# Attention output formed transposed in a pipe of three steps, and the SSD half of the output projection moved ahead of the attention half

## The reference, cut to what matters

```python
def block_attention(q, k, v):            # 8 heads of 64, 2 key/value heads
    s = jnp.einsum('bqkgd,bskd->bkgqs', qi, k).astype(jnp.float32) * scale
    p = jax.nn.softmax(s, axis=-1).astype(v.dtype)
    return jnp.einsum('bkgqs,bskd->bqkgd', p, v)
...
attn = rms_norm(block_attention(q, k, v), attn_norm[i])
ssm = ssm_branch(z, xbc, dt_raw, ...)    # last: y * silu(z), then a grouped rms_norm with gain
x = x + jnp.concatenate([attn, ssm], axis=-1) @ w_out[i]
x = x + moe_ffn(rms_norm(x, norm_ffn[i]), w_router[i], ...)
```

## Time and profile before

| what | value |
|---|---|
| median of 3 runs | 1429.33 us |
| profiled execution, its own time | 1428.61 us |
| span of its records | 1426.8 us |
| TensorE busy | 1316.1 us (92%) |
| VectorE, ScalarE, GpSimd busy | 449.8, 218.2, 191.2 us |
| mean granted TensorE clock | 0.973 of 2.4 GHz |
| read from and written to HBM | 433.30 MB, 14.94 MB |

### The profile page before, as it was taken

How to read it: one execution, slowest core, us unless ns; L and a number is a source line. 1 busy time by engine, 2 the same in 40 slices (tenths; PEclk the granted TensorE clock), 3 DMA queues, 4 the chain that set the end, 5 groups by cost and what they waited for, 6 DMA issues and landing times.

```text
span 1426.8 us, 40195 instructions
## 1 busy us (share of the span) xinstructions
PE 1316.1 (92%) x18053; PEld 811.1 (57%) x18053; DVE 449.8 (32%) x1049; ACT 218.2 (15%) x487; POOL 191.2 (13%) x142
## 2 busy tenths in 40 slices
PE   5999989998799999999998988998999998999973
PEld 3466676665456666666565554655655654666651
DVE  3653577545322222222221221322221321322310
ACT  2132244331101101100110010110010011001100
POOL 0000210000101221111121111121121122012111
PEclk9999999998799999999999999999999999999996
DMA  8000320006999999999999999999999999999992
GB/s 348 4 1 0 148 107 1 31 30 246 384 373 373 394 391 380 403 383 400 395 397 402 396 412 399 407 403 393 411 396 404 406 399 410 389 415 381 407 404 84
DMA packets 79359, 446.18 MB, mean 313 GB/s; under 512 B 13226, under 2 KB 21490, under 8 KB 30034
## 3 DMA queue, kind: packets, MB, share of 16 engines
q1 hardware_dynamic: 63922, 425.85, 74.1%
q0 software_dynamic: 15120, 17.20, 5.7%
q10 hardware_dynamic: 144, 0.52, 0.1%
HBM read 433.30 MB, written 14.94 MB: 314 GB/s over the span
## 4 chain that ended last, share of the span: by engine, by line
SPq 43%; PE 43%; DMA 7%; issue 2%; DVE 2%; POOL 1%; ACT 0%; DVEq 0%; POOLq 0%; ACTq 0%
SPq L609 43%; PE pair L1832 19%; PE pair L1580 7%; DMA ring<-in_w_down 4%; PE pair L1564 4%; PE pair L1541 2%; DMA rest<-in_w_gate 2%; PE pair L1732 2%; PE pair L1672 2%; PE pair L1694 1%; PE pair L1791 1%; POOL ring L711 1%; DMA rest<-normed_rows,rest 1%; DVE rest L1038 1%; PE pair L1767 1%
## 5 line engine op out<-in xcount | busy, mean ns | idle before, releaser
L1832 PE MATMUL pair<-ring,rest 128*32 128x256 f32 x14832 | 847.1, 383 | 44.6 <-DMA ring<-in_w_down 23.6
L1832 PEld LDWEIGHTS pair<-ring,rest 128*32 128x32 f32 x14832 | 479.3, 110 | 358.4 <-issue 29.1
L751 POOL DMA_INDIRECT out<-rest x82 | 128.3, 1565 | 776.8 <-ACT rest L995 722.2
L1038 DVE TENSOR_TENSOR rest<-pair,rest 128x512 f32<-128x512 f32 (+4 forms) x113 | 88.9, 787 | 440.0 <-PE pair L1832 424.5
L995 ACT ACTIVATE rest<-rest 128x256 f32<-128x256 f32 x82 | 36.5, 500 | 541.4 <-DVE rest L1038 541.4
L1580 PE MATMUL pair<-ring 128*128 128x512 f32 (+1 forms) x256 | 99.8, 548 | 1.4 <-DVE ring L1038 0.8
L1580 PEld LDWEIGHTS pair<-ring 128*128 128x128 f32 x256 | 48.9, 193 | 48.3 <-issue 44.7
L1038 DVE TENSOR_TENSOR rest<-rest 128x512 f32<-128x512 f32 (+7 forms) x98 | 62.8, 651 | 32.6 <-ACT rest L977 26.7
L977 ACT ACTIVATE rest<-rest 128x512 f32<-128x512 f32 (+3 forms) x34 | 24.4, 718 | 299.5 <-DVE rest L1367 299.5
L1832 PE MATMUL pair<-rest 128*32 128x256 f32 x912 | 56.2, 384 | 6.5 <-DMA rest<-in_w_down 4.3
L1334 DVE TENSOR_SCALAR rest<-pair 64x1 int32<-64x1 f32 (+3 forms) x34 | 5.2, 152 | 176.0 <-issue 172.4
(11 more groups left out here) (177 smaller groups left out, 873.6 us busy)
## 6 DMA issues: line engine op xcount, KB each, us to landing
ring<-in_w_up SPq DMA_DIRECT2D x121, 1024.0 KB, 28.4
ring<-in_w_gate SPq DMA_DIRECT2D x120, 1024.0 KB, 28.8
ring<-in_w_down SPq DMA_DIRECT2D x120, 1024.0 KB, 29.3
rest<-in_w_gate SPq DMA_DIRECT2D x8, 1024.0 KB, 29.2
rest<-in_w_down SPq DMA_DIRECT2D x8, 1024.0 KB, 29.0
rest<-in_w_up SPq DMA_DIRECT2D x7, 1024.0 KB, 27.8
ring<-in_w_in SPq DMA_DIRECT2D x1, 4160.0 KB, 15.3
ring<-in_x SPq DMA_DIRECT2D x8, 512.0 KB, 6.0
```

Source lines behind the costliest of these rows:

```text
L751: p.indirect_dma_start(out=out_rows, out_offset=bass.IndirectOffsetOnAxis(ap=sidx[vi.ring][:, g:g + 1].bitcast(I32), axis=0), in_=yrow_b[v ...
L1038: return v.tensor_tensor(out=out, in0=a, in1=b, op=op)
L1832: last = T.matmul(ps[q * TOK:(q + 1) * TOK, g * QW:(g + 1) * QW], x, pieces[slot][:, kk, q * QW:(q + 1) * QW], start=(k == 0 and g % 2 == ...
```

## The change

- `attend` swaps the operands: 64 columns of values are stationary and 128 columns of transposed probabilities move; the two heads of a pair go to partitions 0-63 and 64-127 of bank 7, in turns. The attention output so arrives transposed. The pipe has one step more (PT, PV): probabilities are transposed two steps after their scores and used three steps after.
- The sums of the softmax are inverted, spread over 512 columns (`rsq`), transposed by TensorE (`rs`, 4 transposes) and copied out by ScalarE; VectorE multiplies bank 7 by them. The attention norm comes from squares (ScalarE) that TensorE adds with 4 one-column products (`an`); it is applied when VectorE adds the product to x1. The attention gain is multiplied into `w_out`'s first half by GpSimd.
- The output projection is split: the SSD half (`os`, 2 x 4 products) at steps 6, 9, 12, 15, the attention half (`op`, 2 x 4 products) at steps 8, 12, 16, 20. `combine` is at steps 2, 5, 8, 11. x1 is written by two additions per half.
- The sigmoids of z move ahead of the last copy of the SSD stretch, their product with z goes to GpSimd, and `carry_back` goes behind the first maxima. `choose` runs earlier; `th`a is no longer inside `op`b.
- Buffers lie elsewhere, and pieces are issued in another order: 0 to 3 before the loop, 4 to 7 after `yf3` and `op0`, 8 after `th1b`, 9 and 10 after `os3`, 11 and 12 after the last transposes and products of the attention, 13 and 14 after the last x1 tile, 15 and 16 after the last logits. `w_out` comes in two halves, the first behind `w_in`. The stores of the normalized rows are issued by ScalarE.
- Behind the last expert the handling of overflow rows waits in another place; no waiting row is added or taken away for the inputs here.

The diff, cut to its core (indented less):

```diff
-RING_AT = (0, 1, 16, 4, 5, 14, 15, 6, 7, 8, 9, 12, 13, 2, 3, 10, 11)
+RING_AT = (0, 1, 12, 13, 16, 4, 5, 6, 2, 7, 8, 14, 15, 10, 11, 3, 9)
...
-TM, OP, TH, LG = 7, 8, 9, 10
-STEPS = LG + 4 * (NT - 1) + 1
-
-
-def turn_at(s, first):
-
-    t, r = divmod(s - first, 4)
+PT, PV = 2, 3
+YO, TS, OS = 1, 4, 6
+RS, OP, TH, LG = 5, 8, 9, 10
+STEPS = LG + 4 * (NT - 1) + 2
...
+    if n == 2:
+        sp.dma_start(w_out_a, w_out_d[:, 0:KT // 2, :]).then_inc(s_woa, 16)
...
+sp.dma_start(w_out_s, w_out_d[:, KT // 2:KT, :]).then_inc(s_wos, 16)
 for t in range(NT):
     sp.dma_start(x1[:, t, :], x_d[t]).then_inc(s_xr[t], 16)
-sp.dma_start(w_out, w_out_d).then_inc(s_wout, 16)
+wait_full(sp, f"tk{NT - 1}")
...
+load(2, 0)
+load(3, 0)
+
+def store(t):
+
     wait_taken(sp, f"op{t}a")
     wait_taken(sp, f"op{t}b")
     sp.dma_start(out_d[t * P:(t + 1) * P, :], x1[:, t, :]).then_inc(s_ost, 16)
-    if t == NT - 1:
-        for n in range(7, 13):
-            load(n, STREAM[n][1])
-    if t < NT - 1:
-        sp.wait_ge(s_h, t + 1)
-        sp.dma_start(hn_d[t * P:(t + 1) * P, :], hrw).then_inc(s_hst, 16)
+
+store(0)
+sp.wait_ge(s_ys, NT)
+wait_full(sp, f"yf{NT - 1}")
+for n in (4, 5, 6, 7):
+    load(n, STREAM[n][1])
+store(1)
+sp.wait_ge(s_h, 2)
+wait_full(sp, "th1b")
+sp.wait_ge(s_ost, 16 * 2)
+load(8, STREAM[8][1])
+wait_full(sp, f"os{NT - 1}b")
+for n in (9, 10):
+    load(n, STREAM[n][1])
+store(2)
+wait_full(sp, f"p{NPAIR - 1}b")
+load(11, STREAM[11][1])
+sp.wait_ge(s_of, NPAIR)
+load(12, STREAM[12][1])
+store(NT - 1)
+for n in (13, 14):
+    load(n, STREAM[n][1])
 
 sp.wait_ge(s_ost, 16 * NT)
 sp.wait_ge(s_hst, 16 * NT)
 wait_full(sp, f"lg{NT - 1}")
-for n in (13, 14, 15, 16):
+for n in (15, 16):
...
+for n in range(KT // 2):
+    nc.gpsimd.tensor_tensor(out=w_out_a[:, n, :], in0=w_out_a[:, n, :],
+                            in1=pc_att[:, n:n + 1].to_broadcast([P, DM]), op=ALU.mult).then_inc(s_wog, 1)
...
+for c in range(NT):
+    pool.wait_ge(s_zsig, c + 1)
+    nc.gpsimd.tensor_tensor(out=zs[:, c, :], in0=zs[:, c, :], in1=xc[:, c, :], op=ALU.mult).then_inc(s_zg, 1)
...
+    if c == NT - 1:
+        for n in range(NT):
+            nc.scalar.activation(xc[:, n, :], zs[:, n, :], ACT.Sigmoid).then_inc(s_zsig, 1)
...
+    if (i := turn_at(s, RS, 4)) is not None:
+        if i:
+            act.wait_ge(s_ofree, i)
+        copy_out(f"rs{i}", rsT)
+    if (i := turn_at(s, RS + 2, 4)) is not None:
         act.wait_ge(s_ofree, i + 1)
-        link(nc.scalar.activation(junk, mixa, ACT.Square, accum_out=nss[:, 0, i:i + 1]))
-        rms(nrs[:, 0, i:i + 1], nss[:, 0, i:i + 1], AW).then_inc(s_an, 1)
-    if turn_at(s, 3) is not None:
-        i = turn_at(s, 3)
+        nc.scalar.activation(sqT, mixaT[i % 2].rearrange("p a b -> p (a b)"), ACT.Square).then_inc(s_sq, 1)
...
+def carry_back():
+
+    link(tt(by_head(ytmp[0]), by_head(prevb[2]), over(ex[:, 2, 40:48], HD)))
+    link(tt(prevb[1], prevb[1], ytmp[0], ALU.add))
+    link(tt(by_head(ytmp[0]), by_head(prevb[1]), over(ex[:, 1, 40:48], HD)))
+    tt(prevb[0], prevb[0], ytmp[0], ALU.add).then_inc(s_prev, 1)
+    dve.wait_ge(s_prev, 1)
...
+    if (i := turn_at(s, RS + 2, 4)) is not None:
+        wait_taken(dve, f"rs{i}")
+        dve.wait_ge(s_of, 4 * i + 4)
+        if i >= 2:
+            wait_full(dve, f"op{i - 2}b")
+        tt(mixaT[i % 2], cut(bank[7][:, :], NH // 2, P), cut(rsT, NH // 2, P)).then_inc(s_ofree, 1)
+    if (i := turn_at(s, TS, 3)) is not None:
+        dve.wait_ge(s_yn, i + 1)
+        tt(cut(mixs[i % 2], SG, GW), cut(mixs[i % 2], SG, GW), over(nrs[:, 1, i * SG:(i + 1) * SG], GW)
+           ).then_inc(s_mixs, 1)
+    if (i := turn_at(s, TS + 1, 3)) is not None:
+        ps = wait_full(dve, f"ts{i}")
+        if i >= 2:
+            wait_full(dve, f"os{i - 2}b")
+        freed(tt(mixsT[i % 2], cut(ps[:, :], 4, P), over(pc_ssm, P)), f"ts{i}")
+    if (t := turn_at(s, OS + 1, 3)) is not None:
+        dve.wait_ge(s_xr[t], 16)
+        add_rows("os", t, False)
+    if (t := turn_at(s, OP + 1, 4)) is not None:
+        if t == NT - 1:
+            for c in range(t):
+                weigh(c)
+            ps = wait_full(dve, "cue")
+            freed(place(posm[:, 0:t, :], ps[:, 0:t * NE], msk[:, 0:t, :]), "cue")
+            wait_taken(dve, "cue")
+            onehot_tiles(visit_at[0][0], 0, range(t))
+        dve.wait_ge(s_an, t + 1)
+        add_rows("op", t, True)
...
+    if s == 0:
+        carry_back()
+    if 0 <= s - PT < NPAIR:
...
+        v.tensor_copy(by_head(rsq), over(rsum, HD)).then_inc(s_rs, 1)
+    if (i := turn_at(s, YO + 1, 3)) is not None:
+        combine(i)
...
-    for h in range(2):
-        head = 2 * j + h
-        kv = head // (NH // NKV)
-        for kt in range(NT):
-            last = T.matmul(bank[7][:, head * HD:(head + 1) * HD], probsT[p % 2 * 2 + h][:, kt, :],
-                            vs[:, kt, kv * HD:(kv + 1) * HD], start=(kt == 0), stop=(kt == NT - 1))
+    kv = 2 * j // (NH // NKV)
+    for kt in range(NT):
+        for h in range(2):
+            last = T.matmul(bank[7][h * HD:(h + 1) * HD, j * P:(j + 1) * P], vs[:, kt, kv * HD:(kv + 1) * HD],
+                            probsT[p % 2 * 2 + h][:, kt, :], start=(kt == 0), stop=(kt == NT - 1))
     last.then_inc(s_of, 1)
+
+def out_half(u, src, w, h, between=None):
+
+    ps = begin(u)
+    for k in range(KT // 2):
+        if between and k in between:
+            between[k]()
+        last = T.matmul(ps[:, :], src[:, k, :], w[:, k, h * 512:h * 512 + 512],
+                        start=(k == 0), stop=(k == KT // 2 - 1))
+    end(last, u)
+
+def attn_squares(t):
+
+    pe.wait_ge(s_sq, t + 1)
+    ps = bank[where[f"an{t}"][1]]
+    for n in range(NH // 2):
+        last = T.matmul(ps[:, 0:1], sqT[:, n * P:(n + 1) * P], one_c, start=(n == 0), stop=(n == NH // 2 - 1))
+    end(last, f"an{t}")
 
 def before_last_tile():
 
@@ -1693,15 +1773,20 @@
             r = slice(h * HD, (h + 1) * HD)
             end(T.matmul(pss[h][:, :], qT[r, j, i * P:(i + 1) * P], kT[r, 2 * j // (NH // NKV), :],
                          start=True, stop=True), f"s{s}{'ab'[h]}")
-    if 1 <= s <= NPAIR:
+    if 0 <= s - PT < NPAIR:
...
+    if (i := turn_at(s, RS, 4)) is not None:
+        pe.wait_ge(s_rs, i + 1)
+        transposes(f"rs{i}", [rsq[:, n * P:(n + 1) * P] for n in range(NH // 2)])
+    if 0 <= s - PV < NPAIR:
+        attend(s - PV)
+    if (i := turn_at(s, TS, 3)) is not None:
+        pe.wait_ge(s_mixs, i + 1)
+        transposes(f"ts{i}", [mixs[i % 2][:, n * P:(n + 1) * P] for n in range(4)])
...
+    if (t := turn_at(s, OS, 3)) is not None:
+        wait_taken(pe, f"ts{t}")
+        pe.wait_ge(s_wos, 16)
+        for h in range(2):
+            out_half(f"os{t}{'ab'[h]}", mixsT[t % 2], w_out_s, h)
+    if (t := turn_at(s, OP, 4)) is not None:
+        pe.wait_ge(s_ofree, t + 1)
+        pe.wait_ge(s_wog, KT // 2)
+        begin(f"an{t}")
+        out_half(f"op{t}a", mixaT[t % 2], w_out_a, 0, {2: lambda: attn_squares(t)})
         if t == NT - 1:
             before_last_tile()
-        ps = begin(f"op{t}b")
-        for k in range(KT):
-            if k == KT - 2:
-                wait_taken(pe, f"op{t}a")
-                transposes(f"th{t}a", [x1[:, t, n * P:(n + 1) * P] for n in range(4)])
...
```

More of the change, by code:

```diff
@@ L322, in hybrid_layer @@
         kd = cut(qk_w[:, 3 * QKW:], NKV, 2, HD)
-        mixa, mixs, junk = (qk_w[:, n * 512:n * 512 + 512] for n in range(3))
+        mixs = [qk_w[:, n * 512:n * 512 + 512] for n in range(2)]
+        junk, rsq = qk_w[:, 1024:1280], qk_w[:, 1280:1792]
+        wr = cut(qk_w[:, 3 * QKW:], KT, NE)
+        mixaT = [cut(xc_w[:, n * 512:n * 512 + 512], NH // 2, P) for n in range(2)]
+        rsT, sqT = (xc_w[:, n * 512:n * 512 + 512] for n in (2, 3))
+        mixsT = [cut(xc_w[:, n * 512:n * 512 + 512], SH // 2, P) for n in (4, 5)]
         ssq = take(NT); rstd = take(NT)
@@ L379, in hybrid_layer @@
         hrT = cut(ta[:, DM:2 * DM], KT, P)
-        sgx = [ring[:, 23552 + n * 512:24064 + n * 512] for n in range(2)]
-        cbm = cut(ring[:, 23552:24064], 2, SG * P)
-        wr = cut(ring[:, 24064:24064 + KT * NE], KT, NE)
+        sgx = [ring[:, KT * INW + n * 512:KT * INW + n * 512 + 512] for n in range(2)]
+        cbm = cut(ytmp[0], 2, SG * P)
         praw = hTm[:, 0, 0:P]
@@ L1257, in _ @@
                     wait_taken(dve, f"s{4 * i + 3}b")
+                    if i:
+                        wait_full(dve, f"rs{i - 1}")
+                    else:
+                        dve.wait_ge(s_zg, NT)
                     link(v.reciprocal(rsum, sums[:, i % 2, :]))
[L1259 to L1262 removed]
@@ L1276, in _ @@
-                if turn_at(s, OP) is not None:
-                    t = turn_at(s, OP)
-                    if t == NT - 1:
-                        for c in range(t):
-                            choose(c)
-                        for c in range(t):
-                            weigh(c)
-                        ps = wait_full(dve, "cue")
```

(22 more changed lines are left out.)

192 lines of the change are left out of this document (84 added, 108 removed).

## The result

The changed kernel takes 1433.95 us (median of 6 runs, 1431.24 to 1435.20), the kernel before beside it 1428.09 (6 runs, 1425.84 to 1432.25): ratio 1.0034 [1.0022, 1.0046]. I had said 1417, range 1408 to 1430, and given "slower" 0.09. The profiled execution after took 1435.2 us with a span of 1433.3. A T0 comes from one execution, and even the start of the loop differs between executions: with the instruction lists of the kernel before it is at 200.13 and 201.44, with those of the kernel after (edited or not) between 199.66 and 201.70.

A forecast was written before the change was run, and what follows sets the result against it. Bound: TensorE until about 650 us, then the weight stream. Gains of 5.8 (`op3` end), 3.5 (store) and 1.5 (gather) make 10.8, plus 1 for a piece fraction: 11.8 off 1428.6 gives 1416.8; said 1417, range 1408 to 1430.

The forecast's parts named there:

- T0: Start of the first expert product: forecast 361.6 us against 372.4 before; whatever it moves, the whole rest moves.
- the stalls of TensorE in the loop: Steps 7 to 16 of the loop: TensorE's work sums to 86.4 us, plus only 2 for stalls.
- Rival B: Loop: VectorE's in-order list becomes the bound, costing 18 us, for 1435 us; chance 0.10.
- My mark for B: Sign in the loop: TensorE idle over 12 us between 235 and 320 us; the forecast expected under 4.
- The clock: Last tile: the first products of `op3` run at 1.2 GHz, costing 2.2 us.
- `attend`: Loop, each pair: 16 records take 1.23 us, 0.6 us less than before.
- The mode price of 0.14 us: Loop, `attend`: cost of entering the tiling mode, added to 1.09 us for the 16 records.
- Store and gather: Way to the first expert: last rows' store gains 3.5 us (5.2 for 8.7), the gather 1.5.
- GpSimd: Its products delay VectorE: those for z 0 to 1 us, those for `w_out` beside the first rotation 0.
- A: Loop, `attend`: the two heads do not run side by side, 7.7 us lost, 1424.5 us; chance 0.14.
- C: Quicker tail: no clock fall, index binds, gather takes 4 us, no stalls: 1409 us; chance 0.09.
- D: Ends cancel: the loop's start gains nothing and the store still meets four pieces: 1428 us; chance 0.10.

The follow-up runs named there:

- before_tail: Kernel before the change, with pieces 7 to 12 issued only after the last normalized rows have landed: 1429.26 us, ratio 0.9999.
- y_late: Changed kernel with only the products `yf`/`yb` formed one step later, in the step in which `combine` takes them: 1421.63 us, ratio 0.9956.
- lg_first: Changed kernel with the y_late, gain_later and stores_first edits, and VectorE taking the logits ahead of `combine`: 1414.35 us, ratio 0.9904.
- stores_first: Changed kernel with pieces 13 and 14 issued only after the last normalized rows have landed: 1430.21 us, ratio 1.0018.
- gain_later: Changed kernel with GpSimd's gain on `w_out` multiplied between the first and second rotation instead of beside the first: 1431.87 us, ratio 1.0025.

## Why the prediction was wrong, point by point

**That T0 decides: right.** From T0 to the end of the span after and the ten kernels built on it have 1051 to 1054 us, the kernel before 1054.4 (before_tail, with ten pieces held back, 1057.3).

**The step that failed: the stalls of TensorE in the loop** ("the sum 86.4, plus 2 for stalls", and `os0` "at 227.6 to 234.5", where only VectorE's sum and one wait stood). T0 was missed by 19.2 us, and it divides at the marks that I had given:

| up to | forecast | measured | error of the part |
|---|---|---|---|
| end of `os0` | 234.5 | 244.4 | +9.9 |
| end of `op2` | 322.9 | 340.1 | +7.3 |
| end of `op3` | 341.9 | 356.8 | -2.3 |
| first expert product | 361.6 | 380.8 | +4.3 |

17.2 of the 19.2 us lie in the loop. I had summed each engine's work for each stretch and joined the sums only by the data. What joins them as well is the ring of seven banks: a bank stays full until the last engine in line takes it. I had read that a new unit waits for the unit seven before it, and did not follow `yf` and `yb` through it. y_late shows it: with them one step later `op2` ends at 325.3.

**Rival B, given 0.10, was nearest:** I had put it at 1435, and "idle time of TensorE in the loop grows as `attend` shrinks" is what came. But its mechanism was another. I priced VectorE's work in the short steps, 26 us against 29, and argued that two steps of lag hide one long step. In lg_first VectorE has the same work in the same steps, and TensorE is idle for 0.9 of 90 us: the amount of work was no bound, and the lag was enough for the probabilities. What bound was the order in which VectorE took banks, and at the very start `carry_back` ahead of a product of step 1. My mark for B, idle over 12 us between 235 and 320, didn't come: there it was 5.6 of 85, over the forecast's 4; most of the idle time lay before 235, where I had set no mark for it.

**The clock: half of the price was left out.** I charged a fall only once, 2.2 us at the last tile. In the loop after each wait of 1.8 to 3.6 us was followed by products at 1.2 GHz, and in the comparison of after with y_late this cost 8.4 us beside 6.7 of waiting. It isn't so everywhere: in lg_first a wait of 1.97 us was followed by products at full clock. At the last tile itself after ran at full clock (clock 1.00, -2.3 in the table), y_late at the lower.

**`attend`: better than forecast,** 1.02 for 1.23. (The 1.83 that I gave for it before is not what the earlier trace rows show: 233.90 less 232.16 is 1.74; 1.83 it is in other steps, where scores follow. For the sum this is under 0.1 us a pair.) The mode price of 0.14 us that I added does not show. The Trainium skill (TensorEngine Tiling (Array Packing), Key Properties) speaks of a drain at each change; here 16 records with the change into and out of the half arrays take 1.02 us, less than the 1.09 that I had for their loads alone, so if there is one it is hidden in this.

**Store and gather: wrong in size.** Forecast 5.0 us of gain (3.5 + 1.5), measured 0.7. Two pieces ahead delay the rows' store nearly as much as six did (8.1, 8.7). The store of x1, which is issued ahead of it too, does not: in stores_first it is there and the rows' store takes 2.6. And stores_first and before_tail show that 5.5 to 6.0 us off the store bring only 1.1 and 3.1 on the way to T0, since the index then binds and the gather takes longer.

**GpSimd: right.** 5.8 us on VectorE in the rotation, and nothing at the start of the loop (gain_later). The loop starts 1.2 us later than before in the two traces; before_tail, with the lists of the kernel before, starts it 1.3 us later too, so this is within what executions differ by.

**The sum of the change itself came out right, in part by errors that cancel.** With the order mended, no work of the loop taken out, and the two small edits of GpSimd and the pieces, lg_first is at 1414.35 against 1417 forecast, and T0 at 360.33 against 361.6. Its parts miss by +1.9 us (`os0` ends at 236.4), -3.0 (`op2` at 321.8, with the quicker `attend`), -2.4 (`op3` at 338.4, without the fall of the clock that I had charged) and +2.3 (the way to T0, although here the store is quick). What I forecast was the kernel without these waits. Two roundings of the working change nothing: 1416.8 and 0.7 are 1417.5, and the chance of "faster" adds up to 0.72. Of the other rivals, A is false (the heads do overlap), and C and D ask for a loop as I had summed it, which only y_late and the kernels on it have.

## What to carry to other kernels

When units share a ring of PSUM banks in a fixed order, write beside each product the place in the other engine's list where its bank is taken, and count how many units lie between; a product formed a step before a late taker blocks everything behind it, however much slack the data have. Form such a product as late as its taker, or let the small takers go ahead of the long block. A wait can cost more than its length: here 6.7 us of waits came with 8.4 us more for the products, part of which ran at the lower clock, and one wait of 1.97 us came with none. And work saved or added counts in full only where its engine doesn't wait: the same edit of `attend` was worth 2.3 us with the long waits around it and 5.2 without.
